# Where the rest of a search for best keys is run inside an attention stage: behind all thirty-two heads, or behind the first sixteen in double shares

## The reference, cut to what matters

```python
def select_keys(scores, qpos, n_keys, topk):          # topk = 256
    causal = kpos[None, None, :] <= qpos[None, :, None]
    _, idx = lax.top_k(jnp.where(causal, scores, -jnp.inf), topk)
...
def diff_core(q, k, v, qpos, kpos, bias_b, lam, lam_init, subln_g):
    logits = jnp.einsum('bqhcd,bkhcd->bhcqk', q, k).astype(jnp.float32) * (B_HEAD_DIM ** -0.5)
    logits = logits + bias.transpose(2, 0, 1)[None, :, None]
    p = jax.nn.softmax(jnp.where(causal, logits, -jnp.inf), axis=-1)
    w = (p[:, :, 0] - lam * p[:, :, 1]).astype(v.dtype)
    o = jnp.einsum('bhqk,bkhe->bqhe', w, v)
    o = rmsnorm(o, subln_g) * (1.0 - lam_init)
```

## Time and profile before

| | us |
|---|---|
| three timed executions | 2530.52, 2544.35, 2544.56 |
| median | 2544.35 |
| the profiled execution | 2537.31 |
| its span | 2535.5 |
| mean granted clock of PE | 0.972 of full |
| PE busy | 2320.4 (92%) |
| DVE busy | 1080.6 (43%) |
| ACT busy | 736.3 (29%) |
| POOL busy | 687.7 (27%) |

### The profile page before, as it was taken

How to read it: one execution, slowest core, us unless ns; L and a number is a source line. 1 busy time by engine, 2 the same in 40 slices (tenths; PEclk the granted TensorE clock), 3 DMA queues, 4 the chain that set the end, 5 groups by cost and what they waited for, 6 DMA issues and landing times. The chain is left out here.

```text
span 2535.5 us, 32723 instructions
## 1 busy us (share of the span) xinstructions
PE 2320.4 (92%) x12425; PEld 1562.9 (62%) x12445; DVE 1080.6 (43%) x2405; ACT 736.3 (29%) x2025; POOL 687.7 (27%) x731
## 2 busy tenths in 40 slices
PE   7999998876889888888799899989999999999999
PEld 5644444553555555555544345458888888888887
DVE  5479987762355523343313113344433433370001
ACT  3341245653445445444401014211111111100000
POOL 1131121113455455567500010022221222101110
PEclk9999998998999999999999999999999999999999
DMA  4211101005788788877540203101111111122221
GB/s 142 73 63 68 43 1 42 1 1 192 264 319 312 246 313 304 297 222 205 168 151 1 83 24 142 67 36 51 35 51 34 51 35 51 34 78 69 72 65 39
DMA packets 148609, 281.76 MB, mean 111 GB/s; under 512 B 14486, under 2 KB 83782, under 8 KB 148454
## 3 DMA queue, kind: packets, MB, share of 16 engines
q0 software_dynamic: 49408, 176.19, 20.7%
q1 hardware_dynamic: 80758, 90.50, 10.8%
q10 hardware_dynamic: 18288, 12.98, 1.7%
HBM read 261.68 MB, written 17.94 MB: 110 GB/s over the span
## 5 line engine op out<-in xcount | busy, mean ns | idle before, releaser
L629 PE MATMUL PS<-region 128*128 128x512 f32 (+5 forms) x864 | 327.7, 534 | 1.8 <-DMA region<-w_in 1.8
L2659 PE MATMUL PS<-region,ffn_w 128*128 128x264 f32 x1408 | 323.3, 389 | 1.6 <-PEq L2110 1.6
L2659 PEld LDWEIGHTS PS<-region,ffn_w 128*128 128x128 f32 x1408 | 269.8, 192 | 48.1 <-issue 2.0
L629 PEld LDWEIGHTS PS<-region 128*128 128x128 f32 (+1 forms) x864 | 152.9, 181 | 161.0 <-issue 140.7
L1891 ACT COPY region<-PS 128x512 f32<-128x512 f32 x352 | 193.1, 592 | 179.4 <-PE PS L1770 90.1
L2659 PE MATMUL PS<-region,side 128*128 128x264 f32 x1056 | 243.4, 387 | 1.6 <-POOL side L2616 1.6
L2659 PEld LDWEIGHTS PS<-region,side 128*128 128x128 f32 x1056 | 199.2, 190 | 34.7 <-POOL side L2616 1.7
L909 DVE TENSOR_SCALAR_CACHE_REDUCE mask<-score,cand 128x384 bf16<-128x384 f32 (+2 forms) x198 | 180.7, 942 | 4.2
L1770 PE MATMUL PS<-ident_f,region 128*128 128x128 f32 x1024 | 141.7, 281 | 23.6 <-ACT region L1891 21.2
L1640 POOL DMA_INDIRECT region<-cache_b_k,gather_b x128 | 121.2, 947 | 137.7 <-PE PS L1770 115.3
L1640 POOL DMA_INDIRECT region<-cache_b_v,gather_b x128 | 122.4, 956 | 93.7 <-PE PS L1853 59.7
(11 more groups left out here) (430 smaller groups left out, 3833.2 us busy)
## 6 DMA issues: line engine op xcount, KB each, us to landing
ffn_w<-w_gate SPq DMA_DIRECT2D x11, 1024.0 KB, 5.5
ffn_w<-w_up SPq DMA_DIRECT2D x11, 1024.0 KB, 5.5
region<-w_in SPq DMA_DIRECT2D x4, 2048.0 KB, 7.8
ffn_w<-w_down ACTq DMA_DIRECT2D x7, 704.0 KB, 5.6
region<-x_prompt ACTq DMA_DIRECT2D x8, 512.0 KB, 6.8
region<-x_prompt SPq DMA_DIRECT2D x8, 512.0 KB, 10.5
mem_keys<-cache_mem_k SPq DMA_DIRECT2D x8, 512.0 KB, 4.3
mem_values<-cache_mem_v SPq DMA_DIRECT2D x8, 512.0 KB, 8.1
```

What stands on the lines that cost most here:

```text
L629: last = nc.tensor.matmul(M.PS[0:n, s % 3, 0:chunks[j].width], XT[:, c, t * P:t * P + n], w[j % 2][:, c, 0:chunks[j].width], start=(c == 0 ...
L2659: last = nc.tensor.matmul(M.PS[:, bank, 0:TW], left[:, c, :], right[:, c, :], start=begin and c == 0, stop=(c == KH - 1), skip_group_check ...
```

## The change

```diff
@@ -1320,7 +1320,8 @@
                                                    ALU.add).then_inc(comb_done, 1)
                     if n + 2 < N:
                         maxima(n + 2)
-                    M.top.rounds(link, share)
+                    if i < NB // 2:
+                        M.top.rounds(link, 2 * share)
                 M.top.rounds(link, 1e6)
```

## The result

The changed kernel takes 2545.44 us (median of 20 runs, 2537.38 to 2554.03) against 2537.85 for the kernel before (20 runs of the same comparison, 2530.37 to 2544.56). The ratio is 1.0025, with a 95% interval of 1.0013 to 1.0037: **3 to 9 us slower, 6 in the middle** (the medians lie 7.6 apart). The forecast was +4.65, and the time lies in the range.

A forecast was written before the change was run, and what follows sets the result against it. PE, with DVE meeting it at each comb, was taken to bound the short heads, each head's round trip the long ones; 5.5 - 0.7 - 0.15 = +4.65 us gave 2542.0 or 2549.0, forecast between at 2545, range 2533 to 2554.

The forecast's parts named there:

- The short heads, +5.5: Heads 0 to 15: each head's change in search steps, less DVE's wait before the following maxima, sums to +5.5 us.
- Rival 1: Short heads: all steps fit into DVE's waits; +2 us in all, 2539 to 2546; chance 0.2.
- rival 2: Short heads: no step fits, filled waits return as late logits; +11.9 us in all, 2549 to 2556; chance 0.1.
- The milder form of rival 3: First heads: head 0's new wait delays PE's clock rise, each us costing 0.5, up to some 2; called likelier.
- The full form: Short heads: PE's clock stays at 1.2 GHz up to head 16; +33.7 us and more, 2571 to 2578; chance 0.03.
- The long heads, -0.7: Heads from 16: removed scans save 0.26 and 0.43 us, shorter steps nothing, hidden by DVE's wait for logits; -0.7 us.
- Rival 4: Long heads bound by DVE: each removed step shortens its head by its length; -7.1 us, 2530 to 2537; chance 0.06.
- The tail, -0.15: Stage's end: the step before comb(30) goes, but ACT's copies also hold PE; only about 0.15 us comes back.
- A share is 19.67/32: Search work left at the stage's start, 19.67 units, spread over 32 heads: 0.615 per share now, 1.229 after.
- the room left is 0.44: After the change 0.44 of the search's account stays unused, so nothing remains for the call after head 31.
- rival 5: Rounding leaves at most one step, 2 us, for the call after head 31, where nobody waits; changes no number; no chance given.
- `comb(16)` to `comb(31)` "goes from 93.1 to about 92.4": Long heads in the changed profile: the time between these two operations falls from 93.1 to about 92.4 us.

The follow-up runs named there:

- e7: The changed kernel run again on another chip, unaltered: 2691.51 us against 2685.53 for the kernel before, ratio 1.0009.
- e8: Kernel before plus one unread 1.27 us DVE operation after the maxima in each of the 16 short heads: 2695.9 us against 2685.53, ratio 1.0042.
- e10: Kernel before plus one 1.27 us DVE operation behind head 0 only: profiled once, no interval; comb(0) to comb(4) 13.25 us.
- e3: Changed kernel plus one unread 1.27 us DVE operation in each of the 16 long heads: 2693.73 us against 2686.06 for the kernel before, ratio 1.0022.
- e4: Kernel before with PE's turn of a finished block's output issued behind the next head's logits: 2674.17 us against 2686.06, ratio 0.9958.
- e5: Changed kernel with a finished block's output turned behind the next head's logits: 2679.74 us against 2685.53 for the kernel before, ratio 0.9983.
- e1: Kernel before without the search's remaining steps in the differential stage (masks unfinished): 2682.47 us against 2686.06, ratio 0.9993.
- e2: Kernel before with the search's rest in double shares behind the long heads 16 to 31 alone: 2685.89 us against 2686.06, ratio 0.9996.
- e6: Kernel before with the block's turn behind the next head's logits and the search's rest behind the long heads: 2674.39 us against 2685.53, ratio 0.9956.

## Why the prediction was right

- **The sum.** Forecast +4.65 us, measured 3 to 9 with 6.3 in the middle. That the forecast time, 2545, lies within 0.5 us of the measured 2545.44 is luck: it was put between sums on two bases, and on the 2537.85 that the kernel before takes over 20 executions the sum gives 2542.5. The sign came from one comparison: a short head had less wait behind its step than the step was long, a long head had more.
- **The short heads, +5.5.** Heads 0 to 14 were put at 5.25 and measured 6.04 (the change and e7 alike). By piece: heads 0 to 3, 0.95 forecast and 1.2 or 1.3 measured; heads 4 to 14, 4.3 and 4.8 to 4.9. The method, the change of a step less the wait behind it, is within an eighth for the latter, and not because errors cancel. From one end of maxima to the next, heads 0 to 14 changed by +0.94, +0.43, +0.55, -0.41, +0.29, +0.20, 0, +1.05, -0.14, +0.64, +0.32, +0.81, +0.42, +0.94 and -0.01 us in the change's profile. The largest misses are head 1, put at nothing because PE's slow clock sets it, and head 10, put at nothing because its step hardly changes. e8 supports the method with another load: 9.0 us of 21.9 found room. Rival 1 (all fit, +2.8) and rival 2 (none fits, +12.7) are both out by the stage's pieces; the total alone also lies in rival 1's 2539 to 2546. Of the 9.9 us that "can be filled" 0.55 lie before head 0's step, so the low bound was 3.3 rather than 2.8.
- **The milder form of rival 3**, that PE's wait for `comb(1)` puts off the clock's rise, fits e10 and would be in the 1.2; one profile doesn't settle it. The full form did not come: the granted clock is 1.00 in the three pieces after the first.
- **The long heads, -0.7.** The eleven rounds without a turn went from 65.69 to 65.05 and 65.03, -0.65. e3 shows that the reading of the earlier trace rows was right. Rival 4 is out.
- **The tail, -0.15.** Measured -0.02 and -0.05. PE waits 2.31 us there, where it waited 2.34, and the row now names ACT's copy, which was the reason given:

```profile
572.42 1.19 PE L1188 MATMUL PS<-ident_f,region 128*128 128x128 f32 x8 [2.31 <-ACT region L1264]
```

- **"A share is 19.67/32"** was wrong, and with it "the room left is 0.44". The class counts 0.2 for a wait at which the search asks for 0.4, once for each of the three groups, so `time_left` is 0.6 short: 19.07, a share of 0.596 and a double one of 1.192. The last step no longer fits behind head 15. That is rival 5, which had been given no weight in time, rightly: head 15's +0.25 fell away, and the step ran where nobody in the stage waits. `comb(0)` to `comb(16)` takes 58.61 us without that step, where "about 59.6" counted it.
- **`comb(16)` to `comb(31)` "goes from 93.1 to about 92.4"** was wrong in the profile: 96.96, of which 1.1 are the cut and 3.4 the turns' clock. No term stood for the clock after the stalls. In profiles with the change's placement up to head 15 the three turns take 28.97, 28.47 and 26.84 us, in the five others with the old turn 25.59, 25.68, 25.68, 27.25 and 27.53. These overlap, so the falls need no help from the change; that the change makes them a little likelier isn't excluded. e4 against e5 shows that the change's cost doesn't rest on them: without stalls the stage still takes 5.2 us more.
- **The first four heads without a step.** e1 gains 1.9 us there, and e2, with the same instructions in that piece, 3.0. So at least 1.1 us is the clock's moment and not work; I can't split the rest.
- The busiest-engine reading of the Trainium skill ("Perfetto Trace Analysis", section "Optimization Strategy") gave the same sign. The runs agree in part: the stage is longer with the work in the short heads, but e2, which follows the rule, is not measurably faster than before (0.9982 to 1.0011), since the short heads already had almost enough room for single shares.

## What to carry to other kernels

Side work on an engine costs what it exceeds the wait behind it by, place by place. A stage's mean idle share doesn't say that; the waits in order do, and equal rounds with and without a step in the same trace price it directly. Where a steady stall recurs, ask which bank or slot the stalled instruction needs, and whether the next instruction in line needs it too: exchanging the two was worth 12 us here (7 to 15), where the placement of the side work was worth 6 (3 to 9).

## What the hardware showed

- PE's fall to the lower level after a wait of 2.6 us is not settled by the wait. With three waits of 2.6 us (the third 2.9 in e2) the three rounds took 7.45, 9.66 and 10.14 us in e1 and 9.10, 8.01 and 8.57 in e2. One such fall costs 1.4 to 1.7 us against the same round without it (9.10 and 7.45, 9.65 and 8.01, 10.00 and 8.57), once 3.0 (11.60 in e3), and two profiles of one kernel (the change and e7) differ by 2.1 us by this alone.
- The same holds at the stage's end. After PE's last wait for the turn, 2.3 us (3.3 in e2 and e6), the clock fell in ten of the twelve profiles and held 1.00 in e3 and e6, whose ends are 1.5 us shorter than that of the change and 1.4 shorter than that of e2.
- A wait in the stretch before the clock has risen may cost more than itself: in e10, one profile, a piece with one of 0.65 us is 1.7 us longer than in before, whose first piece is the longest without such a wait.
